# Forget-gate query blocks in mixed sequence, and gated low parts placed behind maxima and residual additions

## The reference

```python
def _fox(q, k, v, f_logit, f_bias):        # 4 heads of 64, causal, forget gate
    log_f = log_sigmoid(f_logit + f_bias)
    cum = cumsum(log_f, axis=1)
    for each block of 128 queries:
        sc = q @ k.T * scale + cum_q - cum_k
        sc = where(k_pos <= q_pos, sc, -inf)
        out = softmax(sc) @ v

def first_block(...):
    ya = _mla(...); yb = _fox(...); yc = _chunk_rel(...)
    y = concatenate([_rmsnorm(ya, ga), _rmsnorm(yb, gb), _rmsnorm(yc, gc)])
    x = x + y @ w_o
    x = x + cross attention;  x = x + SwiGLU feed-forward
    return _rmsnorm(x, final_norm)

def swa_sink_mixer(h, kb, vb, pos_bias, mask, w_in, sinks, w_out):
    q, z = split(h @ w_in)                  # 16 heads of 64, 2 key-value heads
    for each block of 128 queries, against 256 keys (band of 128):
        s = where(mask, q @ k.T + pos_bias, NEG_INF)
        m = maximum(max(s), sink)
        p = exp(s - m);  p = p / (sum(p) + exp(sink - m))
        o = p @ v
    return (o * silu(z)) @ w_out

# second block: pool_mixer, then swa_sink_mixer, each x = x + gate * y; rmsnorm at the end
```

## Time and profile before

| | |
|---|---|
| median of three runs | 2364.99 us (2364.39 to 2365.25) |
| profiled execution | 2365.62 us, of which the span of the records is 2363.8 |
| granted TensorE clock, mean | 0.997 |
| TensorE busy | 2325.8 us, 98% |
| VectorE | 1527.3 us, 65% |
| GpSimd | 1253.8 us, 53% |
| ScalarE | 859.7 us, 36% |

### The profile page before, as it was taken

How to read it: one execution, slowest core, us unless ns; L and a number is a source line. 1 busy time by engine, 2 the same in 40 slices (tenths; PEclk the granted TensorE clock), 3 DMA queues, 4 the chain that set the end, 5 groups by cost and what they waited for, 6 DMA issues and landing times.

```text
span 2363.8 us, 32304 instructions
## 1 busy us (share of the span) xinstructions
PE 2325.8 (98%) x11596; PEld 1944.5 (82%) x11596; DVE 1527.3 (65%) x1838; ACT 859.7 (36%) x1596; POOL 1253.8 (53%) x724
## 2 busy tenths in 40 slices
PE   8999999999999999999999999999999999999998
PEld 6888789888887888888888888778888788889877
DVE  6825556524577778877777777773663967057875
ACT  5212555612543222222222443132231344067753
POOL 3533955144145666666777434573745733377733
PEclk9999999999999999999999999999999999999999
DMA  6511011031011333333331111112121123100033
GB/s 219 156 45 46 19 19 37 1 116 45 18 42 50 116 124 116 124 124 121 119 124 62 63 45 45 63 54 72 58 84 53 58 75 132 56 28 28 19 121 129
DMA packets 67324, 178.85 MB, mean 76 GB/s; under 512 B 6978, under 2 KB 13892, under 8 KB 65104
## 3 DMA queue, kind: packets, MB, share of 16 engines
q1 hardware_dynamic: 57744, 147.80, 19.0%
q10 hardware_dynamic: 9104, 27.51, 3.4%
q0 software_dynamic: 368, 2.10, 0.5%
HBM read 161.61 MB, written 15.77 MB: 75 GB/s over the span
## 4 chain that ended last, share of the span: by engine, by line
PE 77%; DVE 5%; issue 3%; POOL 2%; ACT 1%; DMA 0%; DVEq 0%; POOLq 0%; SPq 0%; ACTq 0%
PE ps L701 21%; PE ps L704 21%; PE ps L702 21%; PE ps L851 4%; PE ps L829 3%; PE ps L839 2%; DVE trail L3488 1%; PE ps L2390 1%; POOL split_lo L1645 1%; PE ps L2406 1%; PE ps L2375 1%; PE ps L2376 1%; PE ps L2405 1%; ACT p L952 1%; DVE h_lo L1238 1%
## 5 line engine op out<-in xcount | busy, mean ns | idle before, releaser
L701 PE MATMUL ps<-h_hi,split_hi 128*128 128x512 f32 (+1 forms) x1562 | 612.1, 392 | 14.6 <-DVE h_lo L578 9.1
L702 PE MATMUL ps<-h_lo,split_hi 128*128 128x512 f32 (+1 forms) x1562 | 606.2, 388 | 0.0
L704 PE MATMUL ps<-h_hi,split_lo 128*128 128x512 f32 (+1 forms) x1562 | 541.2, 388 | 0.0
L701 PEld LDWEIGHTS ps<-h_hi,split_hi 128*128 128x128 f32 x1562 | 294.4, 189 | 75.3 <-issue 10.2
L1503 POOL TENSOR_TENSOR split_hi<-raw,cf 128x1024 fp32r<-128x1024 f32 x64 | 124.4, 1944 | 431.8 <-PE ps L704 377.4
L704 PEld LDWEIGHTS ps<-h_hi,split_lo 128*128 128x128 f32 x1562 | 294.2, 188 | 61.5
L702 PEld LDWEIGHTS ps<-h_lo,split_hi 128*128 128x128 f32 x1562 | 294.4, 189 | 56.6 <-issue 0.2
L1592 POOL TENSOR_TENSOR split_lo<-raw,split_hi 128x512 fp32r<-128x512 f32 x144 | 232.6, 1633 | 193.6 <-ACT split_hi L2684 192.0
L1645 POOL TENSOR_TENSOR split_lo<-raw,split_hi 128x512 fp32r<-128x512 f32 x84 | 129.1, 1545 | 178.4 <-ACT split_hi L2845 178.3
L2684 ACT CAST split_hi<-raw 128x512 fp32r<-128x512 f32 x144 | 86.9, 622 | 284.3 <-PE ps L704 205.4
L1505 POOL TENSOR_TENSOR split_lo<-raw,split_hi 128x1024 fp32r<-128x1024 f32 x64 | 177.4, 2772 | 5.0
(11 more groups left out here) (490 smaller groups left out, 5182.2 us busy)
## 6 DMA issues: line engine op xcount, KB each, us to landing
raw<-in_strips SPq DMA_DIRECT2D x208, 256.0 KB, 2.8
raw<-in_strips SPq DMA_DIRECT2D x86, 512.0 KB, 3.5
ada_raw<-in_ada SPq DMA_DIRECT2D x64, 512.0 KB, 3.7
memw_raw<-in_mem_strips SPq DMA_DIRECT2D x8, 512.0 KB, 6.1
xT<-in_xT ACTq DMA_DIRECT2D x4, 1024.0 KB, 7.8
x_spill_d<-xT ACTq DMA_DIRECT2D x1, 3584.0 KB, 10.1
xT<-x_spill_d ACTq DMA_DIRECT2D x2, 1792.0 KB, 10.0
out_T<-out_sb SPq DMA_DIRECT2D x14, 256.0 KB, 2.9
```

What stands on the lines that cost most here:

```text
L701: pe.matmul(acc[:, a:b], w_hi, hi[:, a:b], start=first, stop=False)
L702: pe.matmul(acc[:, a:b], w_hi, lo[:, a:b], start=False, stop=False)
L704: mm = pe.matmul(acc[:, a:b], w_lo, hi[:, a:b], start=False, stop=last)
```

## The change

**Sequence of the fox blocks.** The fox units are built for the blocks 4, 0, 5, 1, 6, 2, 7, 3, and `mix_tokens` follows:

```diff
+FOX_ORDER = [4, 0, 5, 1, 6, 2, 7, 3]
...
-        for t in range(QT):
+        for t in FOX_ORDER:
...
-            return (MLA_ORDER, range(QT), CHK_ORDER)[g // QT][g % QT]
+            return (MLA_ORDER, FOX_ORDER, CHK_ORDER)[g // QT][g % QT]
```

```diff
-        SPLITS = {OUT_FROM - 3: 0, OUT_FROM - 2: 1, OUT_FROM + 1: 2, OUT_FROM + 2: 3, OUT_FROM + 3: 4, OUT_FROM + 5: 5, OUT_FROM + 8: 6}
+        SPLITS = {OUT_FROM - 3: 0, OUT_FROM - 2: 1, OUT_FROM + 1: 2, OUT_FROM + 2: 3, OUT_FROM + 3: 4, OUT_FROM + 5: 5, OUT_FROM + 7: 6}
         LOWS = {m + 1: n for m, n in SPLITS.items()}
-        OUT_PIECES = {0: ((0, 0),), 1: ((0, 1),), 2: ((0, 2),), 3: ((0, 3),), 4: ((1, 0), (1, 1)), 5: ((1, 2), (0, 4)), 6: ((1, 3), (1, 4)),
-                      7: ((0, 5),), 8: ((1, 5),), 9: ((0, 6), (1, 6))}
+        OUT_PIECES = {0: ((0, 0),), 1: ((0, 1),), 3: ((0, 2),), 4: ((0, 3), (1, 0)), 5: ((1, 1), (1, 2)), 6: ((1, 3), (0, 4)),
+                      7: ((1, 4), (0, 5)), 8: ((1, 5),), 9: ((0, 6), (1, 6))}
+        LOWS_BEHIND = ((0, 1, 2, 3), (4,), (5,), (6,), (7,), (), (), ())
...
-                if m in ROWS_AT and rows_in_pair(ROWS_AT[m][0]):
+                if m in ROWS_AT and rows_in_pair(ROWS_AT[m][0]) and m < SWA_PAIRS - 2:
                     swa_rows(*ROWS_AT[m])
                 swa_beside(m)
-                if m in ROWS_AT and not rows_in_pair(ROWS_AT[m][0]):
+                if m in ROWS_AT and not (rows_in_pair(ROWS_AT[m][0]) and m < SWA_PAIRS - 2):
                     swa_rows(*ROWS_AT[m])
...
-                if m in LOWS:
-                    gated_low(dve, LOWS[m])
                 if m + SWA_AHEAD < SWA_PAIRS:
                     swa_maximum(2 * (m + SWA_AHEAD))
                     swa_maximum(2 * (m + SWA_AHEAD) + 1)
...
                 if m >= 0:
                     swa_low(m)
+                if m in LOWS:
+                    gated_low(dve, LOWS[m])
```

```diff
                     act.wait_ge(bout_res, i + 1)
-                    if i == 0:
-                        act.wait_ge(gated_lo, 2 * NK)
                     out_high(n_fin[part], k, k, tok)
-                    if 3 <= i <= 12:
+                    if i == 2:
+                        out_strip_high(act, 6)
+                    elif 4 <= i <= 12:
                         out_strip_high(act, i + 3)
...
-            for n in range(NK, 2 * NK):
-                gated_low(dve, n)
-
...
                                              in1=xT[:, j, tok], op0=ALU.mult, op1=ALU.add).then_inc(bout_res, 1)
+                    for n in LOWS_BEHIND[j] if not part else ():
+                        gated_low(dve, NK + n)
```

## The result

The changed kernel takes 2367.86 us, the median of 22 runs (2365.03 to 2369.54), the kernel before 2364.53 in 22 runs beside it. The ratio is 1.0012, 95% interval 1.0007 to 1.0018: +2.8 us (1.7 to 4.3), and +3.3 between the two medians. That is slower, and within the 0.2% that was called no change. Forecast were 2366.8 us and +1.8. The profiled execution has a span of 2366.4 us against 2363.8.

What follows compares the result with a forecast made beforehand. TensorE was taken to bound the kernel, busy 2325.8 of 2363.8 us, leaving 38 us of idle and slow-clock time. Terms +2.0 - 3.6 + 3.4 = +1.8 gave 2366.8 us against the median of 2364.99; range 2359 to 2370.5.

Steps and rivals of the forecast that it cites:

- Forget-gate: Forget-gate attention in mixed block sequence: changed TensorE waits for exponentials and table loads, +2.0 us, bounds +0.5 and +3.
- The table loads' wait: Forget-gate attention: the wait behind ScalarE's two table loads grows from 0.55 to about 0.85 us.
- The transitions: Forget-gate attention: large units following a small block wait for the exponential at three places, 2.6 us.
- Drain: Start of output projection: first residual ahead of low parts removes the xT wait and slow clock, -3.6 us.
- Pairs' end: End of banded attention: moved low parts collide with GpSimd, 1.8 plus a slow phase of 1.6: +3.4 us.
- 1.35 us gained, if the clock stays up: Pairs' end, first collision: step 58 starts at 2250.1 instead of 2251.45.
- one slow phase of 1.6 us: Pairs' end: TensorE's idling, about 3 of 4 us, brings one slow-clock phase, charged 1.6 us.
- The 0.9 that I added for the weighing of pair 62: Pairs' end: rows' transpose, gate and swa_pt_lo follow the late pieces, another +0.9 us.
- Rival A: Pairs' end: low parts meet GpSimd's gaps and the waits go, -5.7 us there, 2357.7 in all; chance 0.17.
- B: Pairs' end evens out: second collision half as deep, no slow phase, 0 there, 2363.4 us; chance 0.15.
- C: Slower: pairs' end +5, forget-gate +2, late weights cut the drain's gain to 1 us, 2371; chance 0.14.
- D: Forget-gate: mixed sequence hides the exponentials, -1.0 instead of +2.0 us, 2363.8 in all; chance 0.09.

Runs made afterwards that it cites:

- e5: Kernel before with only the forget-gate blocks reordered, to the latent stage's sequence 3, 0, 4, 1, 5, 2, 6, 7: 2365.36 us.
- e6: Kernel before with only the forget-gate blocks reordered, to falling sequence 7 to 0: 2367.37 us, ratio 1.0011.
- e1: Kernel before with the drain's part of the change alone: 2360.92 us, ratio 0.9984.
- e4: e2 with GpSimd's high and low parts of weight strips 1 and 2 made in four instructions each: 2364.84 us.
- e10: e2 with the rows' transpose of step 62 left ahead of its pieces: 2366.93 us, ratio 1.0007.
- e8: e1 with all eight low parts behind the first residual: 2360.26 us, ratio 0.9984.
- e11: Kernel before with only the rows' transpose of step 62 moved behind its pieces: 2365.18 us, ratio 1.0004.
- e12: e8 with the low part ahead of the small sum on VectorE in step 56: 2360.86 us, ratio 0.9984.
- e3: Kernel before with the mixed forget-gate sequence 4, 0, 5, 1, 6, 2, 7, 3 alone: 2366.33 us, ratio 1.0007.
- e2: Kernel before with the pairs' end part of the change alone: 2368.61 us, ratio 1.0012.

## Why the prediction was right

The forecast was +1.8 in the profile's terms, the profiled executions differ by 2.6, and the ratio says 2.8. The stretches name the three parts: mixed +2.2, pairs +4.2, drain -3.9, together +2.5. (The 38 us at the head of the prediction are idle time alone: a matmul at the slow clock counts as busy.)

**Forget-gate.** Forecast +2.0, measured +2.2. The table loads' wait came to 0.82 where 0.85 stood. The transitions are two that wait (0.74 and 0.37, 0.31 and 0.24: 1.66), not three at 2.6; but two small blocks still wait, 0.25 and 0.17, which the forecast had removed, and 0.8 is hidden in matmuls that count as busy. The 2.6 came from a reading of the chunked stage that took all its 2.1 us for transitions; 0.35, 0.33 and 0.21 of them stand before units of small blocks themselves. So the listed waits were forecast about 0.5 too high and the hidden 0.8 was not forecast; that the sum came out at +2.0 is in part luck. e5 and e6 show both mechanisms: a smaller block behind the small one waits less, and the loads alone cost up to 2.48.

**Drain.** Forecast -3.6, measured -3.9. The wait of 1.98 is gone with no other in its place, the split held, the second residual was in time. The starts of the product that waits and of the next one give both terms; the kernel before (the earlier trace rows has the first, 2283.58), then e1:

```profile
2290.72 0.39 PE L701 MATMUL ps<-gated_early,split_hi 128*128 128x512 f32 x1
```

```profile
2280.63 0.39 PE L701 MATMUL ps<-gated_early,split_hi 128*128 128x512 f32 x1
2286.07 0.39 PE L701 MATMUL ps<-gated_early,split_hi 128*128 128x512 f32 x1
```

Behind the last transposes to rows (2271.10 and 2270.30) the first starts at 12.48 and 10.33, so the wait cost 2.15 with its restart; the two starts are 7.14 and 5.44 apart, so the slow phase cost 1.70. Both terms were right to 0.2. e4, e6 and e10 have the wait and no slow phase behind it, and yet take only 0.7 to 1.2 less than the 92.70 of before. In e6 the two starts are 5.52 apart, and then a later product waits for its weights, for which the slow phase had left time:

```profile
2298.58 0.50 PE L702 MATMUL ps<-gated_early,split_hi 128*128 128x512 f32 x1 [0.25 <-POOL split_lo L1686]
```

**Pairs' end.** Forecast +3.4, measured +4.2. Step by step: step 58 was to come 1.35 earlier and came 1.36 earlier (17.95 for 19.31); the last pieces were to start 0.9 later, and it is 0.89 (32.94 us behind step 52 for 32.05). The small operation of 2 us or more near 2258 was 2.36 at 2259.9, the meetings with the port went as worked out, and e4 shows them for what they are. Two things were off.

First, the step "1.35 us gained, if the clock stays up": the number came out, and the forecast said that the slow phase of before is counted in it. It is more than all of it. e8, e6 and e11 have the old order and the old wait of 2.4 us, and take 17.70, less than the 17.95 of the new one. What the change gained there over the profile of before is the slow phase that this profile had and other executions of the same instructions have not. Taken with the clock up, the new order loses 0.25 there. e12 shows how: the small sum, which takes the delay in its place (1.85 us there and in the changed kernel), holds up the row transposes, and TensorE waits 0.84 for them in both. The forecast had worked out the sum's delay, but not the row transposes that need the sum. And that the trace of before had its slow phase there was chance (last section): against one without it, the same step would have read as a loss.

Second, the term "one slow phase of 1.6 us" was mis-sized. TensorE worked some 6 us at 1.2 GHz, 2267.4 to 2273.3, which is about 3 us lost. The 0.9 that I added for the weighing of pair 62 did not come beside it: TensorE's own work took so long that the gate was ready. The two differences, 1.4 more and 0.9 less, leave 0.3 of the 0.8 open.

The rule of the Trainium skill ("SBUF — State Buffer", Who interferes with whom) was the one that spoke against the change, and the runs agree with it at every meeting shown here: VectorE's small operation took 2.36 us under a split of GpSimd, and 0.70 when the split was in quarters. Rival A needed the low parts to meet gaps, and they did not; B's second collision at half depth is what e4 made; C came near in the pairs' end (+4.2 for its +5) but its late split did not come; D is out by e3.

## What to carry to other kernels

Where VectorE and GpSimd both work from SBUF, ask of each moved instruction what GpSimd is in the midst of when it is asked for; a tiny one can cost as much as GpSimd's longest. A wait of the bounding engine is worth its length only if nothing else becomes late in its place: before pricing its removal, follow what takes the delay instead and who needs that. Place first what frees a bank. And measure parts that don't overlap by the distance between the same instructions, where hundredths repeat, not by the total; and ask of each such length whether a slow phase lies in it.

## What the runs showed of the hardware that was not expected

**The clock's fall is not a property of the program.** Seven profiled executions have the same instructions around step 56 and the same wait of TensorE of 2.4 us. In four the granted clock went to 0.50 behind it (before, e1, e3 for 3.4 us, steps 52 to 58 in 19.31 or 19.32; e5 for 6.8, 20.57), in three it did not (e6, e8, e11: 17.70). A price read from one trace at such a place is 0 or 1.6 to 2.9 us, and only several executions say how often. The same holds for the wait for xT of 1.9 to 2.0 us in the drain: behind it the clock fell in five traces (before, e2, e3, e5, e11) and not in three (e4, e6, e10). The executions without a trace fit this: of the changed kernel's 22, the four with a mean granted clock of 0.999 took 2365.5 us on average and the five with 0.996 took 2369.0. Behind the longer idle of the changed order it went down in the changed kernel, e2 and e10, three of three.

**The delay goes both ways.** GpSimd's low part of strip 2 takes 2.85 us in the changed kernel, where it started 0.59 before VectorE's low part ended, and 2.39 in the kernel before, where VectorE had none there. Its high part of strip 1 takes 2.22 in e12, under VectorE's low part, for 1.89.
